# A decoder trunk on one Trainium2 core: its first chunk taken by halves of the inner dimension, its h turned by TensorE, a shorter root, warm-up products on a blank tile, and one weight unit subtracted ahead of a mask

## What is computed

```python
for l in range(DEPTH):
    x = x + 0.5 * swiglu(rms_norm(x, ffn1_norm[l]), ffn1_gate[l], ffn1_up[l], ffn1_down[l])
    h = rms_norm(x, mix_norm[l])
    a_q, ..., c_gate, merge_gate = jnp.split(h @ w_in[l], offsets, axis=-1)
    y_a = dsa_mixer(...); y_b = pool_mixer(...); y_c = nsa_mixer(...)
    g_a, g_b, g_c = jnp.split(jax.nn.sigmoid(merge_gate), 3, axis=-1)
    merged = g_a * (y_a @ proj_a[l]) + g_b * (y_b @ proj_b[l]) + g_c * (y_c @ proj_c[l])
    x = x + merged @ w_out[l]
    x = x + 0.5 * swiglu(rms_norm(x, ffn2_norm[l]), ffn2_gate[l], ffn2_up[l], ffn2_down[l])
return rms_norm(x, final_norm)
# swiglu(x, g, u, d) = (silu(x @ g) * (x @ u)) @ d
```

## Time and profile before

| | us |
|---|---|
| median of 3 runs | 1189.77 (1189.6 to 1189.79) |
| the profiled execution | 1189.75 |
| its span in the trace | 1187.9 |
| PE busy | 1175.4 (99% of the span) |
| DVE busy | 976.4 (82%) |
| ACT busy | 616.1 (52%) |

### The profile page before, as it was taken

How to read it: one execution, slowest core, us unless ns; L and a number is a source line. 1 busy time by engine, 2 the same in 40 slices (tenths; PEclk the granted TensorE clock), 3 DMA queues, 4 the chain that set the end, 5 groups by cost and what they waited for, 6 DMA issues and landing times.

```text
span 1187.9 us, 18888 instructions
## 1 busy us (share of the span) xinstructions
PE 1175.4 (99%) x6442; PEld 967.1 (81%) x6442; DVE 976.4 (82%) x2103; ACT 616.1 (52%) x1045; POOL 74.9 (6%) x151
## 2 busy tenths in 40 slices
PE   8999999999999999999999999999999999999997
PEld 7888888887778888888888888888877888888886
DVE  7988886678878698888788898875889696988886
ACT  6544446556654454444464444465566535444443
POOL 5300000421000000000000000024100000000000
PEclk9999999999999999999999999999999999999999
DMA  9655554553445465455565555535543554655553
GB/s 377 231 188 177 200 190 164 186 178 115 144 178 177 177 212 196 176 209 181 208 219 206 201 187 212 182 142 186 173 148 112 196 194 153 231 191 201 209 179 142
DMA packets 37143, 223.53 MB, mean 188 GB/s; under 512 B 6752, under 2 KB 9440, under 8 KB 11232
## 3 DMA queue, kind: packets, MB, share of 16 engines
q1 hardware_dynamic: 35360, 216.36, 51.4%
q10 hardware_dynamic: 1696, 6.43, 1.6%
q0 software_dynamic: 32, 0.00, 0.0%
HBM read 218.58 MB, written 1.05 MB: 185 GB/s over the span
## 4 chain that ended last, share of the span: by engine, by line
PE 86%; DVE 9%; ACT 3%; issue 2%; DMA 0%; DVEq 0%; ACTq 0%
PE G L1430 21%; PE G L1431 21%; PE G L1432 21%; DVE wlo L960 3%; PE TO L1432 3%; PE TO L1431 3%; PE TO L1430 3%; PE SC L1432 3%; PE SC L1431 3%; PE SC L1430 3%; ACT probs L765 2%; DVE sm L1188 1%; DVE probs L1215 1%; PE TO L1446 1%; PE TO L1707 1%
## 5 line engine op out<-in xcount | busy, mean ns | idle before, releaser
L960 DVE TENSOR_TENSOR wlo<-raw,whi 128x1024 fp32r<-128x1024 f32 x395 | 468.2, 1226 | 114.6 <-ACT whi L579 112.4
L579 ACT ACTIVATE whi<-raw 128x1024 fp32r<-128x1024 f32 x395 | 396.2, 1053 | 266.8 <-PE G L1432 149.2
L1430 PE MATMUL G<-whi,xhi 128*128 128x512 f32 x1184 | 464.4, 392 | 1.2 <-DVE wlo L1023 0.7
L1432 PE MATMUL G<-whi,xlo 128*128 128x512 f32 x1184 | 458.2, 387 | 0.0
L1431 PE MATMUL G<-wlo,xhi 128*128 128x512 f32 x1184 | 458.1, 387 | 0.0
L1430 PEld LDWEIGHTS G<-whi,xhi 128*128 128x128 f32 x1184 | 222.9, 188 | 54.4 <-issue 5.4
L1432 PEld LDWEIGHTS G<-whi,xlo 128*128 128x128 f32 x1184 | 222.8, 188 | 45.6
L1431 PEld LDWEIGHTS G<-wlo,xhi 128*128 128x128 f32 x1184 | 223.0, 188 | 43.3
L1054 DVE STREAM_TRANSPOSE shared_q<-shared_q 32x128 f32<-32x128 f32 x640 | 193.7, 303 | 8.3
L651 ACT ACTIVATE shared_q<-G,stat 128x256 f32<-128x256 f32 x88 | 41.8, 476 | 78.1 <-PE G L1432 75.5
L1430 PE MATMUL TO<-whi,ybhi 128*128 128x512 f32 x176 | 69.0, 392 | 0.0
(11 more groups left out here) (204 smaller groups left out, 968.5 us busy)
## 6 DMA issues: line engine op xcount, KB each, us to landing
raw<-stream SPq DMA_DIRECT2D x200, 1024.0 KB, 4.8
gates<-w_in ACTq DMA_DIRECT2D x2, 2048.0 KB, 8.6
z<-z SPq DMA_DIRECT2D x32, 64.0 KB, 4.2
x<-x_in SPq DMA_DIRECT2D x4, 256.0 KB, 5.8
raw<-stream SPq DMA_DIRECT2D x2, 512.0 KB, 5.7
small<-small_in ACTq DMA_DIRECT2D x2, 414.5 KB, 3.1
const<-const_in SPq DMA_DIRECT2D x1, 690.0 KB, 11.9
z<-zkv SPq DMA_DIRECT2D x32, 16.0 KB, 2.0
```

Of the source, the lines that this page charges most:

```text
L579: act.activation(whi[s][:, c], raw[s][:, c], ACT.Copy).then_inc(hi_done, 1)
L960: dve.tensor_tensor(wlo[s][:, c], raw[s][:, c], whi[s][:, c].bitcast(F32), ALU.subtract).then_inc(lo_done, 1)
L1430: pe.matmul(o, ahi, bhi, start=first, stop=False)
L1432: return pe.matmul(o, alo, bhi, start=False, stop=last)
```

## The change

It has two places. In the **opening** PE no longer waits for the identity: DVE's blanking of `cmp_probs` is put first, and PE multiplies that blank tile by itself eight times (float32 matmuls, no transposes). Of x the first halves of both tiles are loaded first, then unit 0 in two parts, the second halves, and unit 1 in two parts. `first_chunk` lifts half 0 of both tiles, does twenty identity transposes, and then goes by halves of the inner dimension: tok 0 and tok 1 with the first part of unit 0 (with the lift of half 1 of a tile behind each), both with its second part, then tok 0 and tok 1 with unit 1. ACT's squares are four of 128x512 instead of two of 128x1024, and the root is a shorter chain with nothing between its steps. The h of chunk 0 is turned by four PE transposes into `T[0]` ahead of `gate_up(1, 1)` instead of sixteen on DVE. In the **mixer** of both layers, step k = 5 subtracts its unit ahead of the mask.

```diff
-WARM_UP = 2
-KEEP_WARM = 8
+WARM_UP = 8
+KEEP_WARM = 20
...
             load_x(0, 0)
+            load_x(1, 0)
+            load_by_parts(0)
             load_x(0, 1)
-            first = stream[0:1, :, :].rearrange("u p n -> p (u n)")
...
-            load_unit(1, slice(1, 2))
-            load_x(1, 0)
             load_x(1, 1)
+            load_by_parts(1)
             load_unit(2, slice(2, 3))
...
+                    square_half(0, 0, first_squares_done)
                     act.wait_ge(unit_used, 1)
                     lift(l, 0, 0, [0])
-                    act.wait_ge(first_part_in, 16)
+                    act.wait_ge(first_part_in[0], 16)
                     act.activation(whi[0][:, 0:512], raw[0][:, 0:512], ACT.Copy).then_inc(first_hi_done, 1)
                     act.activation(whi[0][:, 512:PART], raw[0][:, 512:PART], ACT.Copy).then_inc(hi_done, 1)
+                    lift(l, 0, 1, [0])
+                    square_half(1, 0, first_squares_done)
                     act.wait_ge(raw_in[0], 16)
                     round_part(0, 1)
                     lift(l, 0, 0, [1])
-                    split(l, at, 1)
-                    square(lift_of(l, 0), 0)
-                    square(lift_of(l, 0), 1)
-                    lift(l, 0, 1)
+                    act.wait_ge(unit_used, 2)
+                    act.wait_ge(first_part_in[1], 16)
+                    round_part(1, 0)
+                    act.wait_ge(raw_in[1], 16)
+                    round_part(1, 1)
+                    lift(l, 0, 1, [1])
+                    square_half(0, 1, squares_done)
+                    square_half(1, 1, squares_done)
...
+                    lift_half(1, 0)
+                    part(0, 1)
+                    lift_half(0, 1)
+                    part(1, 0)
+                    part(1, 1)
+                    lift_half(1, 1)
+                    steps.restart()
+                    dve.wait_ge(first_squares_done, 2)
+                    steps.then(dve.tensor_scalar(ms_part, ss, 1.0 / D, EPS, ALU.mult, ALU.add))
+                    dve.wait_ge(squares_done, 2)
+                    steps.then(dve.scalar_tensor_tensor(ms, ss_rest, 1.0 / D, ms_part, ALU.mult, ALU.add))
...
+                if l == 0 and occ == 0:
+                    split(l, at, 4)
+                    rest_of_h(o * FI + 1, 0, T[0][:, :])
+                else:
+                    turn_h(o * FI)
+                    split(l, at, 4)
+                    rest_of_h(o * FI + 1, 0, by_dve)
...
-                    if k in (1, 3):
+                    if k in (1, 3, 5):
                         split(l, at, 2 * c + 1 + tok)
...
-                    if k > 3:
+                    if k == 4 or k > 5:
                         split(l, at, 2 * c + 1 + tok)
...
+                    for kts in ((0, 1), (2, 3)):
+                        for tok in range(TOKS):
+                            for kt in kts:
+                                ins = products(tok, kt)
+                            if kts[0] == 0:
+                                lift(0, 0, tok, 1)
+                    ins.then_inc(unit_used, 1)
+                    for tok in range(TOKS):
+                        for kt in range(4, KT):
+                            ins = products(tok, kt)
+                        ins.then_inc(unit_used if tok else gu_filled, 1)
...
                 gate_up(1, 0)
+                if l == 0 and occ == 0:
+                    turn_h(o * FI + 1)
                 gate_up(1, 1)
...
+            pe.wait_ge(blank_done, 1)
+            for _ in range(WARM_UP):
+                pe.matmul(SC[0][:, 0:P], cmp_probs[:, :], cmp_probs[:, :], start=True, stop=True)
             pe.wait_ge(first_const_in_sem, 16)
-            for _ in range(WARM_UP):
-                pe.transpose(SC[0][:, 0:P], ident, ident)
```

More of the change, by code:

```diff
@@ L229, in trunk @@
         x_in_sem = [sem(f"x_in_sem{i}") for i in range(2 * TOKS)]
-        first_part_in = sem("first_part_in")
+        first_part_in = [sem(f"first_part_in{i}") for i in range(2)]
         gains_in_sem = sem("gains_in_sem")
@@ L245, in trunk @@
         squares_done = sem("squares_done")
+        first_squares_done = sem("first_squares_done")
         rstd_done = sem("rstd_done")
@@ L362, in trunk, with lift_rank, lift_bank @@
         BY_HALF = [(0, 0), (1, 0), (0, 1), (1, 1)]
+        def lift_rank(l, which, tok, kt):
+            if (l, which) == (0, 0):
+                return kt // 4 * 8 + tok * 4 + kt % 4
+            return tok * 8 + kt
+        def lift_bank(l, which, tok, half):
+            return T[tok if (l, which) == (0, 0) else half]
         def lift_of(l, which):
@@ L467, in _ @@
             pool.dma_start(posi[:, :], pos_in).then_inc(pos_in_sem, 16)
-            for j in range(2 * TOKS):
+            for j in (0, 2, 1, 3):
                 pool.wait_ge(x_in_sem[j], 16)
@@ L606, in lift @@
                 for half in halves:
-                    act.wait_ge(xt_filled, v * 4 + 2 * tok + half + 1)
+                    act.wait_ge(xt_filled, v * 4 + lift_rank(l, which, tok, 4 * half) // 4 + 1)
+                    t = lift_bank(l, which, tok, half)
                     for k in range(4):
@@ L684, in ffn @@
                 split(l, at, 4)
-                round_h(o * FI + 1, 0, by_dve)
+                round_h(o * FI + 1, 0, T[0][:, :] if l == 0 and occ == 0 else by_dve)
                 with act.Fori(1, FI - 1) as i:
@@ L1020, in ffn, with part, lift_half @@
                 if l == 0 and occ == 0:
-                    lift_first(l, 0, range(4))
+                    def part(n, p):
+                        dve.wait_ge(hi_done, part_value(n, p))
+                        subtract_hi(n, p)
+                    def lift_half(tok, half):
+                        for kt in range(4 * half, 4 * half + 4):
+                            lift_tile(l, 0, tok, kt)
+                    dve.wait_ge(gains_in_sem, 16)
+                    lift_half(0, 0)
                     dve.wait_ge(first_hi_done, 1)
@@ L1029, in ffn @@
                     ).then_inc(lo_done, 1)
[L1030 to L1034, removed]
+                    lift_half(1, 0)
[9 more added lines that the diff above has]
+                    steps.then(dve.scalar_tensor_tensor(ms, ss_rest, 1.0 / D, ms_part, ALU.mult, ALU.add))
+                    dve.tensor_scalar(
+                        rs.bitcast(I32), ms.bitcast(I32), -0.5, float(0x5F3759DF), ALU.mult, ALU.add)
+                    steps.then(dve.tensor_scalar(msh, ms, -0.5, None, ALU.mult))
+                    for _ in range(3):
+                        for tok in range(TOKS):
+                            one = slice(tok, tok + 1)
+                            ins = dve.scalar_tensor_tensor(
+                                t1[:, one], rs[:, one], msh[:, one], rs[:, one], ALU.mult, ALU.mult)
+                        steps.then(ins)
+                        steps.then(dve.scalar_tensor_tensor(rs, t1, 1.5, rs, ALU.add, ALU.mult))
+                    dve.tensor_scalar(rs_half, rs, 0.5, None, ALU.mult)
+                    dve.tensor_tensor(rs_sq, rs, rs, ALU.mult).then_inc(rstd_done, 1)
                     dve.wait_ge(hi_done, part_value(2, 0))
@@ L1508, in gate_up, with first_chunk, products @@
                     ins.then_inc(unit_used if tok else gu_filled, 1)
+                def first_chunk():
+                    lift(0, 0, 0, 0)
+                    lift(0, 0, 1, 0)
+                    for _ in range(KEEP_WARM):
+                        pe.transpose(SC[0][:, 0:P], ident, ident)
+                    def products(tok, kt):
+                        a, k, sl = kt // 4, kt % 4, slice(tok * P, (tok + 1) * P)
+                        wait_lifted(0, 0, tok, kt)
+                        if kt == 0:
+                            pe.wait_ge(first_lo_done, 1)
+                        else:
+                            pe.wait_ge(lo_done, part_value(a, k // 2))
+                        c = slice(k * 512, (k + 1) * 512)
+                        return mm3(
+                            G[tok][:, :], xhi[:, kt, sl], xlo[:, kt, sl], whi[a][:, c], wlo[a][:, c], kt == 0, kt == KT - 1)
+                    for kts in ((0, 1), (2, 3)):
[5 more added lines that the diff above has]
+                    ins.then_inc(unit_used, 1)
+                    for tok in range(TOKS):
+                        for kt in range(4, KT):
+                            ins = products(tok, kt)
+                        ins.then_inc(unit_used if tok else gu_filled, 1)
                 def turn_h(n):
```

61 lines of the change are left out of this document (33 added, 28 removed).

## The result

The changed kernel takes 1195.92 us in the median of nine runs, the kernel before 1189.72, also of nine. The means are 1194.77 and 1189.66; their ratio is 1.0043, 95% interval 1.0033 to 1.0052. The two measures differ because the runs of the changed kernel don't lie around their median. They form groups: 1192.62, 1192.63 and 1192.90; one at 1194.50; five from 1195.92 to 1196.15. Nothing like it shows in the runs of before, 1189.19 to 1190.04. The profiled execution, 1196.15 with a span of 1194.4, is one of the upper group, so it can show what the groups are.

What follows compares the result with a forecast made beforehand. The prediction took PE's start, its pace and a few waits to bound the kernel. It summed 1189.75 - 1.1 (opening) + 3.9 (mixer, two layers) = 1192.5 us, own range 1191.5 to 1193.5, whole range 1190.6 to 1195.9.

Runs made afterwards that it cites:

- run 2: The mixer alone: the kernel before with only the mixer's edit (unit 18 ahead of the mask of batch 7, both layers); 1195.08 us, 1.0045 of before.
- run 3: The changed kernel with nine unread float32 128x128 products put ahead of PE's wait for unit 20 in each layer; 1192.70 us, 1.0025 of before.
- run 5: The kernel of run 1 without the eight products on the blank tile; 1190.61 us, 1.0010 of before.
- run 6: The kernel of run 1 without the twenty identity transposes behind the lift; 1190.34 us, 1.0006 of before.
- run 1: The changed kernel with its mixer's order as before (unit 18 behind the mask of batch 7), so the opening alone; 1189.13 us, 0.9995 of before.
- run 4: The changed kernel with step k = 6's top-k round and selection bias moved ahead of `weigh(7)`; 1188.14 us, 0.9986 of before.

## What to carry to other kernels

An instruction that seems to sit in the way of a waiting engine may be the cover of another wait: before moving it, look at what ran on the third engine meanwhile (here ACT's exponentials under DVE's unit 18), and put other work that is ready into its place, as the top-k round was. A wait that is added to a busy TensorE is to be priced twice, once as standing time and once as a possible stretch at half clock behind it, and a median over runs may then lie on a step. When a start is made earlier, ask at each later handover, not only at the next one, whether its other side is earlier too.

## What the runs showed of the hardware

- PE standing for 2.4 us in the middle of full work could let the clock fall to 1.2 GHz (granted clock 1.00 over the wait, 0.57 in the four microseconds behind it), in one place and not in another of the same execution; a fall cost 1.6 us, and with the wait filled by products there was none (the changed kernel, runs 2 and 3).
- Transposes alone raised the clock (run 5: half pace from 4.16, full pace from 10.0), and twenty transposes kept it up that would otherwise have fallen over 2.73 us (run 6).
- The moment of the rise differs between executions of the same opening. The kernel before had its first nine products 0.44 apart; the mixer alone, whose opening is the same, had them at full pace in its profiled execution, behind the same 0.71 us of idle time. PE's timeline there:

```profile
8.85 0.47 PE L1430 MATMUL G<-whi,xhi 128*128 128x512 f32 x1 [0.71 <-DVE wlo L1023]
9.15 0.40 PE L1431 MATMUL G<-wlo,xhi 128*128 128x512 f32 x1
...
33.00 0.50 PE L1430 MATMUL SC<-whi,ybhi 128*128 128x512 f32 x1
```

So a part of what a warm-up gains, the kernel before has already in some of its runs: its first down product is at 33.00 here, against 33.49 in the earlier trace rows and 32.94 to 32.98 with the new opening as a whole (the changed kernel and runs 1, 3 and 4).

- The granted clock is no witness at the start: it reads 1.00 over 5 to 10 us of the kernel before, where transposes are 0.21 and products 0.44 apart. The spacing of equal matmuls shows the pace there.
